# Eighteen blocks of the in-projection in fp32 instead of split fp32r, in a two-layer hybrid decoder step

## The reference

```
proj = x @ w_in                      # 1024 -> 24 tiles of 128 columns: su, hf, hq, hi, rq, rk, rv, hg, rg
o_hg = gated linear recurrence over (silu(hq), hf, hi), normed, times silu(hg)      # HGRN2, 6 heads
o_rt = retention over (rotary(rq), rotary(rk), rv), normed, times silu(rg)          # 6 heads
y5   = S5 scan over su, gelu, gated by a 256x256 linear                             # 16 groups
x = layer_norm(ALPHA * x + concat(o_hg, o_rt, y5) @ w_out)
x = layer_norm(ALPHA * x + square(relu(x @ w_up)) @ w_down)
```

## Time and profile before

| | |
|---|---|
| time before, median of 3 runs | 830.0 us (829.49 to 830.59) |
| the profiled execution's own time | 833.16 us |
| its span, first to last instruction | 831.2 us |
| PE busy | 746.6 us (90%), 7662 matmuls |
| DVE busy | 582.8 us (70%) |
| ACT busy | 417.2 us (50%) |
| mean granted TensorE clock | 0.946 |

### The profile page before, as it was taken

One profiled execution on the slowest core, in us unless ns is written; L12 is line 12 of the kernel. 1 busy time (PEld: TensorE's weight loads), 2 busy tenths in 40 slices (PEclk: granted clock), 3 DMA queues, 4 the chain that ended last, 5 costly groups with the idle time before them and its releaser, 6 DMA issues. The chain is left out here.

```text
span 831.2 us, 18501 instructions
## 1 busy us (share of the span) xinstructions
PE 746.6 (90%) x7662; PEld 711.1 (86%) x7662; DVE 582.8 (70%) x1064; ACT 417.2 (50%) x766; POOL 43.5 (5%) x54
## 2 busy tenths in 40 slices
PE   3779768989999999989997989799899999999994
PEld 3779756878999999989996988687799999999994
DVE  6997996344778899885637789834576886666554
ACT  4736132443577755446436624343456775455432
POOL 4000010200000000000002002010000000000001
PEclk9889897997999999999997989899799999999998
DMA  8442111352435555444542233413143555555631
GB/s 335 146 137 92 53 53 53 131 185 76 149 120 179 162 177 187 166 143 141 178 152 77 80 104 103 143 51 110 56 174 128 178 173 186 184 173 176 201 102 53
DMA packets 31011, 113.61 MB, mean 137 GB/s; under 512 B 3568, under 2 KB 3776, under 8 KB 30544
## 3 DMA queue, kind: packets, MB, share of 16 engines
q1 hardware_dynamic: 28368, 101.83, 36.6%
q0 software_dynamic: 1984, 9.52, 3.0%
q10 hardware_dynamic: 576, 1.08, 0.3%
HBM read 108.24 MB, written 4.18 MB: 135 GB/s over the span
## 5 line engine op out<-in xcount | busy, mean ns | idle before, releaser
L1468 DVE TENSOR_TENSOR w_low<-w_raw,w_high 128x1024 fp32r<-128x1024 f32 x192 | 236.4, 1231 | 151.5 <-ACT w_high L1022 149.1
L1022 ACT ACTIVATE w_high<-w_raw 128x1024 fp32r<-128x1024 f32 x192 | 202.5, 1055 | 239.1 <-PE stream L971 227.7
L969 PE MATMUL stream<-a_high,w_high 128*128 128x264 f32 x768 | 237.1, 309 | 36.1 <-DVE a_low L1473 17.2
L970 PE MATMUL stream<-a_low,w_high 128*128 128x264 f32 x768 | 228.3, 297 | 0.0
L971 PE MATMUL stream<-a_high,w_low 128*128 128x264 f32 x768 | 227.4, 296 | 0.0
L969 PEld LDWEIGHTS stream<-a_high,w_high 128*128 128x128 f32 x768 | 155.5, 203 | 45.2 <-issue 22.7
L970 PEld LDWEIGHTS stream<-a_low,w_high 128*128 128x128 f32 x768 | 155.9, 203 | 0.3
L971 PEld LDWEIGHTS stream<-a_high,w_low 128*128 128x128 f32 x768 | 154.8, 202 | 0.0
L969 PE MATMUL stream<-h_high,w_high 128*128 128x264 f32 x512 | 147.8, 289 | 1.3 <-issue 0.5
L970 PE MATMUL stream<-h_low,w_high 128*128 128x264 f32 x512 | 145.1, 283 | 0.0
L971 PE MATMUL stream<-h_high,w_low 128*128 128x264 f32 x512 | 145.0, 283 | 0.0
(11 more groups left out here) (371 smaller groups left out, 971.9 us busy)
## 6 DMA issues: line engine op xcount, KB each, us to landing
w_raw<-in_weights SPq DMA_DIRECT2D x192, 512.0 KB, 3.3
mats<-in_matrices POOLq DMA_DIRECT2D x2, 1024.0 KB, 5.2
S_hg<-in_state_hg POOLq DMA_DIRECT2D x2, 768.0 KB, 4.9
out_hg_s<-S_hg POOLq DMA_DIRECT2D x2, 768.0 KB, 3.7
consts<-in_constants POOLq DMA_DIRECT2D x1, 1484.5 KB, 9.3
X<-in_xT ACTq DMA_DIRECT2D x4, 264.0 KB, 5.7
out_y<-X SPq DMA_DIRECT2D x4, 264.0 KB, 2.1
S_rt<-in_state_rt POOLq DMA_DIRECT2D x2, 512.0 KB, 6.6
```

The lines of the kernel that those rows point to most:

```text
L969: pe.matmul(bnk[:, 0:width], wh, xh, start=(first and kk == 0), stop=False)
L970: pe.matmul(bnk[:, 0:width], wh, xl, start=False, stop=False)
L1022: act.activation(w_high[:, n % SPLIT_SLOTS, :], w_raw[:, n % RAW_SLOTS, :], ACT.Copy).then_inc(high_ready, 1)
L1468: put(tt(w_low[:, n % SPLIT_SLOTS, :], w_raw[:, n % RAW_SLOTS, :], w_high[:, n % SPLIT_SLOTS, :].bitcast(F32), ALU.subtract), low_ready)
```

## The change

`UNSPLIT` names eleven in-projection blocks of layer 0 (0, 1, 4, 6, 8, 10, 12 to 16) and seven of layer 1 (6, 8, 10, 12, 14, 15, 16). For these, `split_high` and `split_low` return at once, and PE multiplies `w_raw` with `X` in fp32, 8 matmuls a block. The counters of the splits count split blocks alone. A raw buffer of such a block is free for SP's next load when PE has done the block, no longer when DVE has done its split. At the start SP's load of block 1 waits for the second quarter of x, GpSimd's three memsets for the mixers move behind its four loads, and DVE does the second piece of the S5 tables ahead of the split of x.

```diff
+UNSPLIT = ((0, 1, 4, 6, 8, 10, 12, 13, 14, 15, 16), (6, 8, 10, 12, 14, 15, 16))
+SPLIT = [_n % N_CHUNKS not in UNSPLIT[_n // N_CHUNKS] for _n in range(DEPTH * N_CHUNKS)]
+FIRST_SPLIT = [min(_c for _c in range(N_CHUNKS) if _c not in UNSPLIT[_l]) for _l in range(DEPTH)]
...
-        def wait_low(eng, n):
-
-            eng.wait_ge(low_ready, n + 1)
+        def split_count(n):
+
+            return sum(SPLIT[:n + 1])
+
+        def wait_raw(eng, n):
+
+            eng.wait_ge(raw_loaded[n % RAW_SLOTS], 16 * (n // RAW_SLOTS + 1))
+
+        def wait_raw_read(eng, n):
+
+            if SPLIT[n]:
+                eng.wait_ge(low_ready, split_count(n))
+            else:
+                eng.wait_ge(chunk_done, n + 1)
...
-                if n == 2:
-                    sp.wait_ge(x_loaded[3], 16)
+                if n in (1, 2):
+                    sp.wait_ge(x_loaded[2 * n - 1], 16)
                 if n >= RAW_SLOTS:
-                    wait_low(sp, n - RAW_SLOTS)
+                    wait_raw_read(sp, n - RAW_SLOTS)
...
-            pool.memset(near[:, :, :, :, :], 0.0).then_inc(cleared, 1)
-            pool.memset(st_p[:, :, :], 0.0).then_inc(cleared, 1)
-            pool.memset(level_space, 0.0).then_inc(cleared, 1)
             pool.wait_ge(x_loaded[1], 16)
             pool.dma_start(mats[:, :], matrices[0]).then_inc(mats_loaded, 16)
...
             pool.dma_start(s5x0[:, :, :, :, :], state_s5).then_inc(const_loaded, 16)
+            pool.memset(near[:, :, :, :, :], 0.0).then_inc(cleared, 1)
+            pool.memset(st_p[:, :, :], 0.0).then_inc(cleared, 1)
+            pool.memset(level_space, 0.0).then_inc(cleared, 1)
...
-                    wait_low(pe, n)
+                    if SPLIT[n]:
+                        pe.wait_ge(low_ready, split_count(n))
+                    else:
+                        wait_raw(pe, n)
+                if not SPLIT[n]:
+                    if l:
+                        pe.wait_ge(x2_ready, 8 * l)
+                    for k in kks:
+                        if n == 0 and k % 2 == 0:
+                            pe.wait_ge(x_loaded[k // 2], 16)
+                        mm = pe.matmul(bnk[:, 0:T], w_raw[:, n % RAW_SLOTS, 128 * k:128 * k + 128], X[:, k, :], start=(k == 0), stop=(k == 7))
+                    mm.then_inc(chunk_done, 1)
+                    return
...
-                        if c in (0, OUT0, UP_B):
-                            pe.wait_ge(a_ready, 24 * l + 8 * (0, OUT0, UP_B).index(c) + kk + 1)
+                        if c in (FIRST_SPLIT[l], OUT0, UP_B):
+                            pe.wait_ge(a_ready, 24 * l + 8 * (FIRST_SPLIT[l], OUT0, UP_B).index(c) + kk + 1)
...
-                if n >= DEPTH * N_CHUNKS:
+                if n >= DEPTH * N_CHUNKS or not SPLIT[n]:
                     return
-                act.wait_ge(raw_loaded[n % RAW_SLOTS], 16 * (n // RAW_SLOTS + 1))
+                wait_raw(act, n)
                 if n >= SPLIT_SLOTS:
                     act.wait_ge(chunk_done, n - SPLIT_SLOTS + 1)
...
-                if n >= DEPTH * N_CHUNKS:
+                if n >= DEPTH * N_CHUNKS or not SPLIT[n]:
                     return
-                dve.wait_ge(high_ready, n + 1)
+                dve.wait_ge(high_ready, split_count(n))
...
-            pieces(1)
+            pieces(2)
             split_low(0)
             for m in range(KT):
                 split_a(0, 0, m, X, m)
             split_low(1)
-            pieces(1)
```

## The result

The changed kernel takes 837.7 us (median of 8 runs, 833.5 to 843.4), the kernel before 830.3 in the same session (8 runs, 828.1 to 832.9): a ratio of 1.0083, 95% interval 1.0054 to 1.0112, so slower by 7 us. The forecast was 827.2 us with a range of 820.5 to 832.5: wrong in sign, and outside the range. The profiled execution took 837.68 us (span 835.6). One execution each in experiments 3 and 7, and one of the kernel before beside experiments 1 to 4 (1894.5 us), count as slow: the medians include them, the ratios do not.

A forecast was written before the change was run, and what follows sets the result against it. DVE was taken to bound layer 0's first half and layer 1 from 475 us, PE the stretch from 128 to 197 us. Layer 0's gain of 7.3 and layer 1's loss of 4.5 gave 830.0 - 2.8 = 827.2 us, range 820.5 to 832.5.

The forecast's parts named there:

- The hidden part, the mechanism: Weight loads, both layers: a split block's load now waits for PE's raw block three ahead; low half 4.45 us after, before 1.15.
- Layer 1 so loses 4.5 us: Layer 1's mixers: late loads and lowered clock outweigh the dropped splits; loss 4.5 us, bounds 0 and 9.
- no earlier than 4.45 us after the end: Split block behind a raw one: landing 3.3, high half 1.06, hand-overs 0.1 put its low half at least 4.45 us later.
- half of it is won back by dropped split 110: Layer 1 after low 109: half of its 2.1 us lateness is regained because DVE no longer splits block 110.
- a third of the price: Layer 1, lowered TensorE clock: two places, each at a third of 3.55 us, counted as 2 x 1.15 = 2.3 us.
- The second rival: Layer 1: raw blocks 104 and 106 both at lowered clock, 3.55 us each, loss 9.3, total 832.0 us; chance 0.20.
- Layer 0, start: Kernel start: DVE saves a 1.30 us wait and two splits, 3.6 us; first low half at about 17.0 us.
- the table piece that is moved ahead costs the same in either place: Layer 0's start, DVE: doing the second S5 table piece ahead of the split of x adds no time.
- GpSimd's memsets lie in its idle time: Layer 0's start: the memsets moved behind GpSimd's loads fall where it is idle; no cost was counted.
- Layer 0, tables: Layer 0's tables: dropped splits bring low 9's lead to 5.4 us, PE's to 6.0, sum 7.3, bounds 4.7 and 9.
- The price of an fp32 block: PE, each raw block: 3.55 us at 2.4 GHz, 0.65 more than a split one; 11.8 us for 18 blocks.
- The first rival: Both layers: loads do not bind; layer 0 gives about 8.2, layer 1 some 3.5, total 818.3 us; chance 0.12.

The follow-up runs named there:

- experiment 3: Kernel before, all blocks split, only SP's loads into seven layer 1 blocks' slots held until PE has done those blocks: 852.7 us, ratio 1.0211.
- experiment 7: Changed kernel, with loads 106, 108, 110, 112 and 116 held back until the load ahead of each has landed: 837.2 us, ratio 1.0056 against the kernel before.
- experiment 1: Changed kernel with layer 0's eleven fp32 blocks alone, layer 1 all split: 827.5 us, ratio 0.9950 against the kernel before.
- experiment 2: Changed kernel with layer 1's seven fp32 blocks alone, layer 0 all split: 848.9 us, ratio 1.0203 against the kernel before.
- experiment 4: Changed kernel, all eighteen fp32 blocks loaded into the `w_low` slots of their numbers instead of `w_raw`: 821.8 us, ratio 0.9868 against the kernel before.
- experiment 5: Changed kernel with layer 1's seven fp32 blocks alone, loaded into slots of their own: 829.5 us, ratio 0.9969 against the kernel before.

## Why the prediction was wrong, step by step

**The hidden part, the mechanism: right.** The high halves named in the prediction are released by the load, DVE is idle 3.87 and 6.46 us before lows 107 and 109, and experiments 3, 4 and 5 show that this wait is the cause: put in alone it makes a loss, and shortened under the same fp32 products it takes the loss away.

**"Layer 1 so loses 4.5 us": the step that failed.** The term was mis-sized; it measured 12.6 in the profile, and over executions about 11 us (1.0083 against 0.9950 for layer 0 alone). Since layer 0 gave 4.2 us over executions instead of 7.3, about two thirds of the miss of some 10 us is layer 1's and a third layer 0's. Two things were too small in layer 1's term.

First, the chain "no earlier than 4.45 us after the end". It was 4.85 us for low 107 (479.48 to 484.33), 6.2 for low 109 (492.64 to 498.81) and 5.7 for low 115. Its 3.3 us for the landing came from a kernel in which the median is 3.3; in the changed one it is 3.7, and 5.0 and 4.6 for 109 and 115, which ran beside the load behind (107's ran beside one too, and landed in 3.7).

Second, what follows. In the time of the kernel before (layer 1 entered 8.2 us earlier), low 107 came 1.1 us late where I had 0; block 106 ended 2.7 us late, 1.5 of it because it ran at a lowered clock (4.96 us between its first and last start instead of 3.44); with 1.7 more for the landing, low 109 was 6.5 us late instead of 2.1. Then "half of it is won back by dropped split 110" did not come: block 112 ended 9.5 us late instead of 3.1, low 115 was 9.9 late instead of 2.2, and block 118 at a lowered clock took the last 1.5.

The clock in block 106 of the change, and in the same block without the late loads:

```profile
487.30:492.64 5.34, 5.34 (x31) 4.10 (x32) 4.58 (x10) 0.00 (x0) 0.00 (x0) 0.71 0.00 0
```

```profile
484.06:487.89 3.83, 3.83 (x35) 3.03 (x34) 3.42 (x8) 0.00 (x0) 0.00 (x0) 1.00 0.78 265
```

A late split can so cost twice: by the pause, and by the clock behind it, which makes the next fp32 block end later, and the next load with it. Block 106 had a mean clock of 0.54 to 0.71 in five of the seven profiles in which low 107 came late, behind a pause of 3.9 to 4.6 us, and of 1.00 in all seven in which it did not (pause 0.9). In the other two late ones (104 alone, and one load at a time; pauses 3.9 and 3.8) it was 1.00 as well, so a lowered clock there is frequent and not certain. The prediction gave the clock "a third of the price" at two places and kept the waits apart from it. The second rival (both raw blocks at 1.2 GHz, 832.0 us) had this mechanism; in the profile it met block 106, in part, but not 104, in the version with 104 alone it met most of 104. It too was short, since it held the waits at 2.2 us. The Trainium skill, "TensorE: Matmul & The Clock Gate", section Loop structure matters more than you think, warned of a wait for a transfer between bursts of matmuls, behind which they run cold: these rows agree, 0.71 behind a late load and 1.00 in its absence; the two profiles named above do not.

**Layer 0, start: half right.** The first low half is DVE's in block 2:

```profile
14.24 2.84 DVE L1499 TENSOR_TENSOR a_low<-X,a_high 128x264 fp32r<-128x264 f32 x8
...
18.79 1.23 DVE L1494 TENSOR_TENSOR w_low<-w_raw,w_high 128x1024 fp32r<-128x1024 f32 x1
```

It came at 18.8 us, not at 17.0, so 1.75 us earlier than before instead of 3.6; its load had landed at 16.62. What is missing was lost ahead of the split of x, in the step "the table piece that is moved ahead costs the same in either place" and in "GpSimd's memsets lie in its idle time". In the moved piece one small DVE operation, of a kind that takes 0.17 us, took 4.77 us, and ended with the last of the moved memsets; before, one took 3.10 us beside the memsets in their old place. First the change, then before:

```profile
9.00 4.77 DVE L1527 TENSOR_SCALAR par<-par 128x8 f32<-128x8 f32 x1
11.06 2.68 POOL L522 MEMSET scratch<- 128x3072 f32 x1
```

```profile
4.50 3.10 DVE L1485 TENSOR_SCALAR par<-par 128x8 f32<-128x8 f32 x1
4.90 2.68 POOL L502 MEMSET scratch<- 128x3072 f32 x1
```

So DVE stood still 1.7 us longer than before, which is nearly all of the missing 1.85. In all fourteen profiles such an operation ends 0.03 to 0.04 us behind the last memset; no run moved the memsets alone.

**Layer 0, tables: the sum right, not its parts.** Low 9, its split released by a load:

```profile
45.82 1.23 DVE L1494 TENSOR_TENSOR w_low<-w_raw,w_high 128x1024 fp32r<-128x1024 f32 x1 [1.63 <-ACT w_high L1048]
```

Its lead is 3.7 us, not 5.4, again with a chain of 5.1 us instead of 4.45. The rest was made good by the clock: block 9 ran at 2.88 us between first and last start where it had taken 5.80 before. So PE's first table unit came 5.85 us earlier (6.0 forecast), and the first S5 half scan 7.17 us (7.3):

```profile
59.81 1.94 PE L587 MATMUL mix<-consts,scratch 128*128 128x128 f32 x16 [0.41 <-DVE scratch L1615]
```

```profile
86.79 0.69 DVE L1634 TENSOR_TENSOR scratch<-mix,rot 128x512 f32<-128x512 f32 x1
```

That this is partly chance shows in the seven profiles with the same layer 0: where block 9 ran slower (4.06, 4.87 and 4.93 us), the lead behind layer 0 was 4.8, 2.5 and 0.6 us, in the other four (2.88 to 3.70 us) 5.9 to 7.7. That the profile of the change had 7.4 is luck. Over executions layer 0's part is worth 4.2 us (ratio 0.9950, 1.8 to 6.6) rather than 7.3.

**The price of an fp32 block: right.** Block 110 took 3.83 us from its first start to its end (515.81 to 519.64), the split one before 3.16: 0.67 us more, where 0.65 was forecast (18 of these are 11.7 us, not the 11.8 of the prediction).

**The first rival** (the loads do not bind, 818.3 us) described experiment 4, which takes most of the binding away: ratio 0.9868, or 819 us on the prediction's scale. Its parts are not confirmed: in the profile, the slowest of four executions, layer 0 gave 8.3 us and layer 1 0.2, where the rival had 8.2 and 3.5.

## What to carry to other kernels

When an operation is removed that was also what freed a buffer, look up who frees it now and what follows from there: transfer, copy, split, and the work behind them. Give a stage that is fed late the whole chain, with the landing time of loads that run together and a possible lowered clock behind each pause, since the delays feed one another: by the ratios, one late load already cost about half of what six did. And where blocks of two kinds share a ring of buffers, try giving each kind slots of its own before judging the change: here the same eighteen products went from 0.8% slower to 1.3% faster.

## What the runs showed of the hardware that was not expected

Every version with fp32 blocks (7 to 18 of them) had its 512 KB weight loads land in 3.7 or 3.8 us (median), and also in the stages where nothing was changed: 3.6 to 4.0 between 640 and 800 us (3.7 in the change), against 3.3 there in the kernel before. The versions without fp32 blocks, with late loads or with the start edits alone, had 3.3 over all loads (between 640 and 800 us 3.5 and 3.3). Slots of their own did not change it (3.7, and 3.8 for the fp32 blocks). The bytes and the packets on the queue are the same. What makes the loads slower was not found.

A small DVE operation of 0.17 us lasted as long as GpSimd's memsets ran beside it, 3.1 us before and 4.6 to 4.9 us where they were moved, in every profile.

The times of most versions spread by 8 to 14 us between executions (the changed kernel 833.5 to 843.4 us, at granted clocks from 0.961 down to 0.941), while the kernel before kept to 6.5 us in 31 runs, layer 0 in its own slots to 1.8 in 5 and the start edits alone to 5.3 in 10: one profile is a poor measure of a version that spreads so.
